# Six of an MLP's last eight output tiles in seven products of blocks in place of eight, with the memory keys' statistics placed in its first quarter

## The reference, cut to what matters

```python
def _sq_relu_mlp(h, w1, w2):
    return jnp.square(jax.nn.relu(h @ w1)) @ w2      # 1024 -> 4096 -> 1024
...
y_x = _sq_relu_mlp(_modulate(x, g_pre_mlp[l], sh2, sc2), w_mlp_in[l], w_mlp_out[l])
x = x + gt2 * _rmsnorm(y_x, g_post_mlp[l])
```

## Time and profile before

| | us |
|---|---|
| median of 3 runs (lowest, highest) | 1289.29 (1289.21, 1289.40) |
| the profiled execution, its own time | 1289.89 |
| its span in the trace | 1288.6 |

### The profile page before, as it was taken

The page is one execution under the profiler, slowest core; times in us unless marked ns, Lnnn a source line. Parts: engine busy times, 40 slices in busy tenths (PEclk is TensorE's granted clock), DMA queues, the critical chain, the costliest instruction groups (busy, mean ns, idle before and its releaser), DMA issues.

```text
span 1288.6 us, 22877 instructions
## 1 busy us (share of the span) xinstructions
PE 1279.2 (99%) x8718; PEld 1137.5 (88%) x8718; DVE 962.9 (75%) x1692; ACT 782.5 (61%) x1488; POOL 808.7 (63%) x585
## 2 busy tenths in 40 slices
PE   9999999999999999999999999999999999999998
PEld 6787778879999999988788788777789999999998
DVE  5796795878778989834478575747589887987888
ACT  4532586478677584855655547645577655765664
POOL 2643333679778687656467372644378876877785
PEclk9999999999999999999999999999999999999999
DMA  9685335353333333523332112111123323333333
GB/s 378 239 313 212 91 130 215 121 180 99 115 108 107 108 99 99 180 99 112 118 114 83 44 55 73 59 66 36 64 82 116 99 99 107 106 100 116 99 107 107
DMA packets 42125, 156.35 MB, mean 121 GB/s; under 512 B 4384, under 2 KB 5152, under 8 KB 40992
## 3 DMA queue, kind: packets, MB, share of 16 engines
q1 hardware_dynamic: 41136, 151.60, 34.1%
q0 software_dynamic: 448, 2.62, 0.5%
q10 hardware_dynamic: 432, 0.67, 0.1%
HBM read 149.90 MB, written 4.19 MB: 120 GB/s over the span
## 4 chain that ended last, share of the span: by engine, by line
PE 84%; DVE 8%; ACT 3%; POOL 2%; issue 2%; DMA 0%; DVEq 0%; POOLq 0%; ACTq 0%
PE bank L879 23%; PE bank L881 22%; PE bank L880 22%; PE bank L1437 2%; PE bank L928 1%; PE bank L930 1%; PE bank L929 1%; PE bank L982 1%; DVE small L2940 1%; PE bank L1153 1%; PE bank L975 1%; PE bank L1134 1%; PE bank L942 1%; PE bank L967 1%; PE bank L1674 1%
## 5 line engine op out<-in xcount | busy, mean ns | idle before, releaser
L3809 POOL TENSOR_TENSOR wL<-raw,wH 128x1024 fp32r<-128x1024 f32 (+1 forms) x91 | 224.6, 2473 | 239.4 <-ACT wH L1815 236.3
L879 PE MATMUL bank<-hH,wH 128*128 128x512 f32 (+1 forms) x544 | 211.0, 388 | 1.2 <-POOL wL L3809 0.6
L881 PE MATMUL bank<-hH,wL 128*128 128x512 f32 (+1 forms) x544 | 200.6, 369 | 0.0
L880 PE MATMUL bank<-hL,wH 128*128 128x512 f32 (+1 forms) x544 | 200.4, 368 | 0.0
L3814 POOL TENSOR_TENSOR wL<-raw,wH 128x512 fp32r<-128x512 f32 (+1 forms) x120 | 154.4, 1287 | 31.1 <-ACT wH L1824 30.5
L879 PE MATMUL bank<-gH,wH 128*128 128x256 f32 x512 | 145.4, 284 | 0.6 <-POOL gL L3814 0.6
L881 PE MATMUL bank<-gH,wL 128*128 128x256 f32 x512 | 144.9, 283 | 0.0
L880 PE MATMUL bank<-gL,wH 128*128 128x256 f32 x512 | 144.9, 283 | 0.0
L1815 ACT ACTIVATE wH<-raw 128x1024 fp32r<-128x1024 f32 (+1 forms) x91 | 95.1, 1047 | 53.3 <-PE bank L881 26.9
L879 PEld LDWEIGHTS bank<-hH,wH 128*128 128x128 f32 x544 | 102.9, 189 | 24.5 <-issue 6.7
L881 PEld LDWEIGHTS bank<-hH,wL 128*128 128x128 f32 x544 | 102.6, 189 | 18.0
(11 more groups left out here) (538 smaller groups left out, 4073.0 us busy)
## 6 DMA issues: line engine op xcount, KB each, us to landing
raw<-in_wall SPq DMA_DIRECT2D x211, 512.0 KB, 3.3
rows<-in_wall SPq DMA_DIRECT2D x24, 1024.0 KB, 11.4
bra<-in_rpbw SPq DMA_DIRECT2D x8, 360.0 KB, 3.1
xq<-in_xt SPq DMA_DIRECT2D x2, 1024.0 KB, 6.7
xT<-in_xn SPq DMA_DIRECT2D x1, 2048.0 KB, 7.7
out_x<-xT SPq DMA_DIRECT2D x1, 2048.0 KB, 8.6
xT<-out_x SPq DMA_DIRECT2D x1, 2048.0 KB, 9.3
out_x<-xT SPq DMA_DIRECT2D x6, 256.0 KB, 2.4
```

Source lines behind the costliest of these rows:

```text
L879: matmul(o, a_h, b_h, start=first, stop=False)
L880: matmul(o, a_h, b_l, start=False, stop=False)
L881: return matmul(o, a_l, b_h, start=False, stop=last)
L3809: tt(wL[i % NHL][:, 0:n], raw[load(c) % NRAW][:, 0:n], wH[i % NHL][:, 0:n].bitcast(F32), ALU.subtract).then_inc(s.w_lo, 1)
```

## The change

Output tiles 0 to 5 of the last quarter become three outer pairs, 12, 13 and 14, by the same scheme as the other quarters; tiles 6 and 7 stay plain. Chunks 12 to 15 therefore get their sums of forms, and the second half of the even hidden tiles is kept aside (`xlast`) and split once by ACT (`late_high`) and POOL for tiles 6 and 7. Output results are squared (`result_square`) and summed (`result_sum`) as they are finished, from outer pair 13 on. The keys' statistics become two of 512 columns (two heads each) and stand behind the first product of outer pair 3 and of inner pair 2; the lower bounds go to outer pairs 0, 1, 2 and 4, the second step of the angles from outer pair 7 to 6. x is read back in two halves after the last product of the last pair, and these transfers stand on SP ahead of the third chunk of the next weights (`first_f + 2`).

```diff
-OUT_ORDER = [24 + i for i in (0, 1, 2, 3, 4, 5, 7, 6)]
+OUT_ORDER = range(24, 32)
+Y_ORDER = (1, 0, 3, 2, 5, 4)
...
-             + [("outer", 4 * quarter + j) for j in range(4 if quarter < 3 else 0)]]
+             + [("outer", 4 * quarter + j) for j in range(4 if quarter < 3 else 3)]]
...
+    of.update({("mk", i): of["sum", OUTER[2 + i], 1] for i in range(2)})
...
@@ tensor_program
+        KEY_PLACE = {(OUTER[3], 0): 0, (INNER[2], 0): 1}
+        def memory_statistic(i):
+            statistic_of_halves(f"mk{i}", 512, BANK["mk", i])
+            freed[BANK["mk", i]] = s.mk_n, 2 * i + 2
...
+                if (n, q) in KEY_PLACE:
+                    memory_statistic(KEY_PLACE[n, q])
...
-        for m in range(6):
-            b = BANK["w_mlp_out", m]
-            if m >= 2:
-                tile("w_mlp_out", m, OUT_ORDER, [(claim(b), XB)])
-            freed[b] = s.y_full, m + 1
-            if 0 < m < 5:
-                statistic_of_halves(f"mk{m - 1}", 256)
...
@@ scalar_program
+        def late_high():
+            act.wait_ge(s.relu_sq, 2 * 15)
+            act.wait_ge(s.prod, 7 * (INNER[13] + 1))
+            copy(xlH[:, :, :], xlast[:, :, :], s.full)
+        def memory_squares():
+            act.wait_ge(s.k_mem, 4)
+            activation(ksq[:, :], kvM[:, 0:2, :].rearrange("p a t -> p (a t)"), ACT.Square).then_inc(s.head_sq, 4)
+            act.wait_ge(s.head_sq, 4)
+            activation(ksqH[:, :], ksq[:, :], ACT.Copy).then_inc(s.sums_hi, 2)
+        def result_square(i):
+            act.wait_ge(s.y, Y.half + 24 + i + 1)
+            if i > 2:
+                act.wait_ge(s.add_g, ADD_G.f + i - 2)
+            square((ysq[i % 2] if i else ysum)[:, :], y[:, Y_ORDER[i], :], s.sq)
...
+            if not more:
+                first_product(n)
+                ahead("w_mlp_out", OUT_ORDER[0], 6, 2)
+                result_square(2)
+                result_square(3)
+                continue
...
+            if n in (OUTER[3], INNER[2]):
+                memory_root(n - OUTER[3])
             piece_high(n + 1, 2)
-            if c is not None and c < 12:
+            if c is not None:
                 sums_of_form_high(c, 0)
+            if outer_of(n) == 13:
+                late_high()
             piece_high(n + 1, 3)
...
+            if outer_of(n) == 13:
+                result_square(0)
+                result_square(1)
...
+            if outer_of(n) == 0:
+                memory_squares()
+            if outer_of(n) == 2:
+                act.wait_ge(s.lb_v, 3)
+                activation(lb[:, 1, :], lb[:, 1, :], ACT.Exp).then_inc(s.lb_a, 1)
+                activation(lb[:, 2, :], lb[:, 2, :], ACT.Exp).then_inc(s.lb_a, 1)
...
@@ vector_program
             if n + 1 < G:
                 piece_low(n + 1, 2)
+            if n in (OUTER[3], INNER[2]):
+                memory_key(n - OUTER[3])
             product_sums(n)
...
-            if outer_of(n) in (5, 7, 9, 10):
+            if outer_of(n) in (5, 6, 9, 10):
                 next(turn_)
+            if outer_of(n) in (0, 1, 2, 4):
+                next(bound)
...
@@ gpsimd_program
+        def result_sum(i):
+            pool.wait_ge(s.sq, SQ.f + i + 1)
+            if i > 1:
+                pool.wait_ge(s.add_g, ADD_G.f + i - 1)
+            tt(ysum[:, :], ysum[:, :], ysq[i % 2][:, :], ALU.add).then_inc(s.add_g, 1)
...
             if n + 1 == G:
-                ahead("w_mlp_out", 24, 0, 2)
+                result_sum(1)
+                ahead("w_mlp_out", OUT_ORDER[0], 6, 2)
+                result_sum(2)
+                result_sum(3)
                 continue
...
             piece_rest(n + 1, 3)
+            if outer_of(n) == 13:
+                pool.wait_ge(s.full, FULL.b + 33)
+                rest(xlL[:, :, :], xlast[:, :, :], xlH[:, :, :], s.rest_g)
...
+            if outer_of(n) == 1:
+                pool.wait_ge(s.sums_hi, halved("mk1") + 1)
+                tt(ksqL[:, :], ksq[:, :], ksqH[:, :].bitcast(F32), ALU.subtract).then_inc(s.sums_lo, 2)
+        result_sum(4)
+        result_sum(5)
...
         late_squares(0)
+        ahead("w_mlp_out", OUT_ORDER[0], 6)
...
@@ sync_program
-            if i == last_inner:
-                sp.wait_ge(s.prod, outer_done(2))
+            if i == first_f + 2:
+                sp.wait_ge(s.prod, 7 * G)
                 sp.wait_ge(s.x_moved, 32)
-                nc.sync.dma_start(xT[:, :, :], out).then_inc(s.x_moved, 16)
+                nc.sync.dma_start(xT[:, 0:4, :], out[:, 0:4, :]).then_inc(s.x_moved, 16)
+                nc.sync.dma_start(xT[:, 4:8, :], out[:, 4:8, :]).then_inc(s.x_rest_in, 16)
             weights_load(i)
```

More of the change, by code:

```diff
@@ L96, in plan_weights @@
                 tile("w_mlp_in", m + i, range(odd, 8, 2))
[L97 to L104, removed]
+        for j in range(4 if quarter < 3 else 3):
+            for i, odd in ((0, 0), (1, 0), (1, 1), (0, 1)):
+                tile("w_mlp_out", 2 * j + i, range(8 * quarter + odd, 8 * quarter + 8, 2))
+    for m in (6, 7):
+        tile("w_mlp_out", m, OUT_ORDER)
     wide("w_in_2", 14, range(8))
@@ L952, in statistic_of_halves @@
             matmul(o[:, 0:n], ones_r[:, :], low, start=False, stop=True).then_inc(s.summed, 1)
-            freed[7] = s.root, logged(name)
+            freed[b] = s.root, logged(name)
         def four_sums(b, squares, first, half):
@@ L1327, in tensor_program, with XB @@
             first_freed(n)
[L1329 to L1340, removed]
-        for m in range(6):
-            b = BANK["w_mlp_out", m]
-            if m >= 2:
-                tile("w_mlp_out", m, OUT_ORDER, [(claim(b), XB)])
-            freed[b] = s.y_full, m + 1
-            if 0 < m < 5:
-                statistic_of_halves(f"mk{m - 1}", 256)
+        def XB(k, i):
+            c = 12 + (k - 24) // 2
+            if k % 2:
+                return yH[:, c % 4, 256 + 256 * i:512 + 256 * i], yB[c % 4][:, i, :], s.lo, LO.b + 2 * c + 1
+            if i:
+                return xlH[:, c % 4, :], xlL[:, c % 4, :], s.rest_g, REST_G.b + 33
+            return yH[:, c % 4, 0:256], yA[c % 4][:, :], s.lo, LO.b + 2 * c + 2
         freed[2] = freed[3] = s.piece_v, 2 * G
@@ L1354, in half_statistic @@
             pe.wait_ge(s.sq, SQ.f + 8 + 2 * i)
-            matmul(o, ones[:, :], acc[0][:, 256 * i:256 * i + 256], start=True, stop=False)
+            matmul(o, ones[:, :], ysum[:, 256 * i:256 * i + 256], start=True, stop=False)
             matmul(o, ones[:, :], tm[3][:, 256 * i:256 * i + 256], start=False, stop=True).then_inc(s.summed, 1)
@@ L3229, in added, with memory_key, lower_bounds @@
             tt(y[:, m, :], y[:, m, :], sum_bank(n, (1, 3)[count - 1]), ALU.add).then_inc(s.y, 1)
+        def memory_key(i):
+            dve.wait_ge(s.root, rooted(f"mk{i}"))
+            dve.wait_ge(s.ones, 5)
+            stt(out=kvM[:, i, :], in0=kvM[:, i, :], scalar=vc("mem_k"), in1=bank[BANK["mk", i]],
+                op0=ALU.mult, op1=ALU.mult).then_inc(s.mk_n, 2)
+        def lower_bounds():
+            l0, l1 = vcs("lb0"), vcs("lb1")
+            dve.wait_ge(s.mod_late, 4)
+            tt(coef[:, 4, :], mod[:, 40:48, 0], vcs("g_post_mlp"), ALU.mult).then_inc(s.coef_c, 1)
+            yield
+            tt(lb[:, 0, :], l0, l1, ALU.max).then_inc(s.lb_v, 1)
+            dve.wait_ge(s.lb_v, 1)
+            tt(lb[:, 1, :], l0, lb[:, 0, :], ALU.subtract).then_inc(s.lb_v, 1)
+            yield
+            tt(lb[:, 2, :], l1, lb[:, 0, :], ALU.subtract).then_inc(s.lb_v, 1)
+            yield
+            dve.wait_ge(s.lb_a, 2)
+            tt(lb[:, 0, :], lb[:, 1, :], lb[:, 2, :], ALU.add).then_inc(s.lb_v, 1)
+            dve.wait_ge(s.lb_v, 4)
+            nc.vector.reciprocal(lb[:, 0, :], lb[:, 0, :]).then_inc(s.lb_v, 1)
+            dve.wait_ge(s.lb_v, 5)
+            tt(lb[:, 3, :], lb[:, 1, :], lb[:, 0, :], ALU.mult).then_inc(s.lb_v, 1)
+            dve.wait_ge(s.lb_v, 6)
+            ts(lb[:, 2, :], lb[:, 3, :], -1.0, 1.0, ALU.mult, ALU.add).then_inc(s.lb_v, 1)
+            yield
+        bound = lower_bounds()
         plain_squares()
@@ L3958, in gpsimd_program @@
             piece_rest(n + 1, 6)
-        for m in range(8):
-            if m not in (1, 7):
-                ahead("w_mlp_out", OUT_ORDER[4 if m == 0 else 0], m)
-            if 0 < m < 6:
-                if m > 1:
-                    pool.wait_ge(s.add_g, ADD_G.f + m - 1)
-                add_squares(acc[0][:, :], m, s.sq, SQ.f)
+            if outer_of(n) == 1:
[3 more added lines that the diff above has]
+        result_sum(5)
         def late_squares(i):
```

184 lines of the change are left out of this document (58 added, 126 removed).

## The result

The median of 22 runs is 1291.47 us, beside 1289.39 for the kernel before in as many: **2.08 us slower** (0.16%), ratio 1.0015 with an interval of 1.0009 to 1.0022. The forecast was 1.58 us faster, and the range ended at 1290.3. The profiled execution took 1291.26 us, 1.26 of it outside its span of 1290.0.

The account below looks back on a forecast made before the run. TensorE (PE), busy 99% of the span, was taken to bound the kernel. -33.71 + 30.24 + 0.91 + 0.68 + 0.20 + 0.10 = -1.58 us, so a median of 1287.71 us; range 1286.4 to 1290.3.

Parts of the forecast that it names:

- the price of the lower bounds' steps: Outer pair 4: four dependent VectorE steps take 0.68 us, not hidden, and lengthen the stall before outer pair 9: +0.68.
- another one: Skill's TensorE issue-gap rule: narrow matmul 98 ns, 75% of a wide one, a loss of 5.8 us; set aside for the trace.
- the angle step: Second angle step moved to outer pair 6 puts inner pair 6's weight pieces behind it: 0 to 0.7 us, taken as 0.
- POOL's queue at the end: From the last pair's start, POOL needs 17.3 to 17.7 us; PE asks at 17.64: 0 to 0.5, taken as 0.
- Three pairs: Replacing output tiles 0 to 5: 3 x 84 narrow matmuls at 0.120, 30.24 us, where the old stretch took 33.71.
- The statistics: Keys' statistics in outer pair 3 and inner pair 2: 0.91 us of matmuls, plus 0.10 waiting for their bank.
- The mechanism at the head of the third quarter: VectorE's lag grows from 3.70 to 4.38, so the stall before outer pair 9 grows from 0.25 to 0.93 us.
- the unoffset case: Last quarter keeps a lag of 4.01 at inner pair 13, a stall of about 0.6; waits then total 1.48 us.
- the offset: PE being 0.68 later cuts the last quarter's lag from 4.01 to 3.33; its first two pairs take 10.18 each, +0.20.
- No new wait: Rival: VectorE's arrears are absorbed, giving -2.56 us and 1286.7; chance 0.20.
- x comes too late: Rival: x's reload lands past tile 6's start + 10.2 us, the next norm waits, 1291.7; chance 0.12, 0.07 over 0.2% slower.
- Narrow matmuls: Rival: in the new pairs a narrow matmul costs 0.159 us, 9.8 more in all, giving 1297.5; chance 0.01.

Follow-up runs that it names:

- both steps were moved: Changed kernel with the lower-bounds steps at outer pair 3 and the second angle step at outer pair 7; median 1287.70 us, 2.02 below the kernel before.
- the first experiment: Changed kernel with the last four lower-bounds steps at outer pair 3 instead of 4; median 1288.17 us, 1.55 below the kernel before.
- the last version: Changed kernel with lower bounds at outer pair 3, two result sums on VectorE, angle steps two each at outer pairs 5 and 9; 1287.39 us, ratio 0.9982.

## Why the prediction was wrong

**Where it failed: the price of the lower bounds' steps.** The prediction wrote "561.53 to 562.21, 0.68 us" and carried it to outer pair 4. It knew that VectorE is in arrears there and that PE would pay one for one, and both held; but it took the price from a place where POOL had nothing to do, and gave it no upper bound. It was 3.44. With that one number replaced the prediction's own sum is -1.58 + 2.76 = +1.18. The rows of before bound it: POOL's instructions beside the pairs take 1.30, three steps that may each wait for one make up to 3.9. The place of the wait was right only in part: the prediction puts all of it before outer pair 9, where 1.04 came, while 2.70 came in outer pair 7 and inner pair 6, on VectorE's own low parts.

The Trainium skill, "SBUF — State Buffer", section "Who interferes with whom", has this rule: a VectorE instruction with two inputs in SBUF contends with a GpSimd instruction that reads SBUF; one in a mode that uses both ports, which a tensor_scalar can enter, does so too, and whoever issues first has the shared pair of ports for the whole instruction; one with at most one SBUF input, outside those modes, does not contend. The runs agree: the two tensor_tensor steps and the tensor_scalar took 1.00 to 1.22 beside POOL and 0.15 to 0.17 without it, the reciprocal 0.18 both times. In which mode the tensor_scalar ran, no trace shows. It is a rule that spoke against the change, and the prediction weighed another one.

**A second, smaller term: the angle step.** "Adds nothing to DVE's total within those arrears" was off by 0.47 (4.68 against 4.21); that POOL is the cause here too is argued from the 2.14 that the same step takes in POOL's pause. 0 to 0.7 had been kept as bounds. That it "puts inner pair 6's weight pieces behind it" was right as a place: that is where PE waited. It decided where the wait fell, not how long it was.

**POOL's queue at the end** cost 0.51, the upper end of "0 to 0.5", where I took 0. The half-sum ended at 600.21, 18.05 behind the start of the last pair, not 17.3 to 17.7: the prediction let POOL's instructions follow at once or overlap by 0.05, but the last result sums, which need one another, stood 0.14 apart (four of 1.30 took 5.62):

```profile
593.72 5.62 POOL L3930 TENSOR_TENSOR ysum<-ysum,ysq 128x512 f32<-128x512 f32 x4
```

**What held.** Three pairs at 84 x 0.120, 30.43 with the two starts of 10.18 (30.24 + 0.20 said). The statistics, 0.96 together (0.91 + 0.10 said), without a gap before them. The mechanism at the head of the third quarter: VectorE's lag at inner pair 9 was 474.42 - 469.69 = 4.73, 1.03 above the 3.70 of before, and outer pair 8 grew by 1.04. In the last quarter, the unoffset case is borne out where both steps were moved and nothing is added ahead: the lag at inner pair 13 was 4.00 (4.01 said), and outer pair 12 took 10.64, a stall of 0.46 (0.6 said). The difference is a slip of reading: the 0.25 of stall in the third quarter of before is 0.17 in the earlier trace rows (10.35 against 10.18), so PE waits once the lag passes 3.53, not 3.45. It cancels in the +0.68. In the changed kernel 4.73 - 3.53 gives 1.20, and outer pair 8 took 11.39 - 10.18 = 1.21 more than an unstalled pair in its place.

**What came out by luck: the offset.** The changed kernel's lag at inner pair 13 was 3.29, where 4.01 - 0.68 = 3.33 was said, and outer pair 12 took 10.18. But 3.29 is also the lag that VectorE has without arrears, as in the second quarter of before, and the prediction's road is only part of the way there: PE was 1.04 later, and the third angle step happened to take 3.56 us in place of 4.24. In the first experiment PE was 0.47 later and the lag was 4.01 all the same, since that step took 4.70 there. No run separates the two.

**The rivals.** "No new wait" is not the changed kernel, but the last version comes within 0.05 of its sum up to tile 6. "x comes too late" did not happen: both halves were issued by 592.80 and landed 5.1 and 7.9 us after their issue, by 600.7, and VectorE's first add of x, at 602.92, had no idle time before it. The kernel did become slower, by 0.16%, within the 0.2% that the prediction counts as no change, and not by that road. Narrow matmuls kept 0.120.

Added up against the traces: -3.28 + 0.96 + 3.85 + 0.51 = +2.04, beside +2.08 in the medians. The profiled executions differ by only 1.37, because 0.24 and 0.40 fell away in stretches that the change does not touch (0.3 of it at the one wait of the second MLP). That 2.04 meets 2.08 so closely is luck: executions of either kernel lie up to 0.7 apart.

## What to carry to other kernels

The price of a small VectorE instruction is not its own: read what POOL does at the place it moves to, and bound it by one POOL instruction per step. An engine in arrears hands every added microsecond to the engine that waits for it, and the wait that the trace then names tells where the queue ran dry, not who filled it; so compare the busy time put in with the wait that came out, before moving what is named. Seven products in place of eight pay only while a narrow matmul costs under 48/84 = 0.57 of a wide one; at 0.120/0.227 = 0.53 the whole gain here was 2.5 us, and four misplaced steps of 3.4 us together undid it.

## What the runs showed of the hardware

Four instructions on 128x4 elements took 3.44 us beside POOL and 0.67 in a pause, a factor of five. The wait goes the other way as well: beside the second angle step two of POOL's splits, 1.30 otherwise, took 1.62 and 1.74 in the changed kernel:

```profile
433.70 1.62 POOL L3813 TENSOR_TENSOR pL<-raw,pH 128x512 fp32r<-128x512 f32 x1
435.28 1.74 POOL L3813 TENSOR_TENSOR wL<-raw,wH 128x512 fp32r<-128x512 f32 x1
```

The granted clock was 1.00, its upper level, in every stretch shown.
